# Reordering weight loads, a late scales load and the last tile's routing in a hybrid decoder step

## The reference, cut to what matters

```python
def hier_moe(m, w_router_group, w_router_expert, w_gate, w_up, w_down):
    # top-1 of 4 groups, then top-2 of its 8 experts, per token
    ...
    hg = jnp.einsum('btd,edf->btef', m, w_gate)      # 32 experts, 1024 -> 256
    hu = jnp.einsum('btd,edf->btef', m, w_up)
    hidden = jax.nn.silu(hg) * hu * gates[..., None].astype(m.dtype)
    return jnp.einsum('btef,efd->btd', hidden, w_down)

def decoder_layer(...):
    ...
    h = h + mixed
    h = h + hier_moe(rms_norm(h, g_ffn), *ffn_w)
    gate = jax.nn.sigmoid(jnp.einsum('btd,de->bte', rms_norm(h, g_ple), w_ple_gate))
    h = h + jnp.einsum('btp,pd->btd', p_i, w_ple_proj) * gate
```

## Time and profile before

| | |
|---|---|
| Median of three runs | 1237.9 us (1232.99 to 1240.14) |
| Profiled execution | 1235.65 us, span 1233.9 us |
| TensorE products busy | 1147.6 us, 93% of the span |
| TensorE weight loads | 593.5 us, 48% |
| VectorE / ScalarE / GpSimd | 407.2 / 323.6 / 144.8 us |
| Granted TensorE clock, mean | 0.971 |
| DMA | 224.17 MB, mean 182 GB/s |
| Chain that ended last | TensorE 83%, DMA 8%, VectorE 3%, ScalarE 2% |

### The profile page before, as it was taken

How to read it: one execution, slowest core, us unless ns; L and a number is a source line. 1 busy time by engine, 2 the same in 40 slices (tenths; PEclk the granted TensorE clock), 3 DMA queues, 4 the chain that set the end, 5 groups by cost and what they waited for, 6 DMA issues and landing times.

```text
span 1233.9 us, 14797 instructions
## 1 busy us (share of the span) xinstructions
PE 1147.6 (93%) x5706; PEld 593.5 (48%) x5706; DVE 407.2 (33%) x968; ACT 323.6 (26%) x635; POOL 144.8 (12%) x141
## 2 busy tenths in 40 slices
PE   6999997999999999999999998789998887889997
PEld 3444443666666665554555555324443332234443
DVE  0222223566651332132256554361111111024443
ACT  2232322677721121110111112211111100134443
POOL 0111010012220000000101111331321100000000
PEclk9999998999999999999999997899999988899999
DMA  8211013111074436334487226449999996982431
GB/s 307 58 51 51 21 39 91 48 36 35 2 217 142 118 113 171 120 120 149 150 313 265 109 83 259 166 166 410 416 418 415 410 418 257 404 310 89 156 125 39
DMA packets 69940, 224.17 MB, mean 182 GB/s; under 512 B 17822, under 2 KB 31550, under 8 KB 54000
## 3 DMA queue, kind: packets, MB, share of 16 engines
q1 hardware_dynamic: 59264, 194.26, 43.8%
q0 software_dynamic: 9888, 26.37, 5.7%
q10 hardware_dynamic: 720, 2.62, 0.5%
HBM read 196.62 MB, written 31.32 MB: 185 GB/s over the span
## 4 chain that ended last, share of the span: by engine, by line
PE 83%; DMA 8%; DVE 3%; ACT 2%; issue 2%; SPq 1%; POOL 0%; ACTq 0%; POOLq 0%; DVEq 0%
PE pair L1898 14%; PE pair L2110 13%; PE pair L2309 9%; PE pair L2173 9%; PE pair L2407 9%; DMA R<-in_w_up 6%; PE pair L2331 4%; PE pair L1967 3%; PE pair L1954 3%; PE pair L1980 3%; PE pair L2202 1%; PE pair L2029 1%; PE pair L2296 1%; PE pair L2046 1%; PE pair L2388 1%
## 5 line engine op out<-in xcount | busy, mean ns | idle before, releaser
L2309 PE MATMUL pair<-R 128*32 128x512 f32 (+2 forms) x896 | 159.8, 630 | 26.8 <-DMA R<-in_w_up 24.7
L2110 PE MATMUL pair<-R 128*128 128x352 f32 x576 | 178.6, 463 | 0.0
L1898 PE MATMUL pair<-R 128*128 128x512 f32 x384 | 171.8, 605 | 3.3 <-DMA R<-in_w_in 3.3
L2110 PEld LDWEIGHTS pair<-R 128*128 128x128 f32 x576 | 106.6, 190 | 57.9 <-issue 4.4
L1898 PEld LDWEIGHTS pair<-R 128*128 128x128 f32 x384 | 73.3, 194 | 91.0 <-issue 91.0
L2173 PE MATMUL pair<-R 128*128 128x512 f32 x256 | 115.3, 604 | 0.0
L2407 PE MATMUL pair<-R 128*128 128x512 f32 x256 | 111.5, 593 | 1.7 <-ACT R L1216 1.7
L2309 PEld LDWEIGHTS pair<-R 128*32 128x32 f32 (+2 forms) x896 | 51.9, 130 | 119.6 <-issue 115.9
L1721 DVE TENSOR_TENSOR R<-pair,R 128x256 f32<-128x256 f32 x21 | 8.9, 425 | 235.4 <-ACT R L1173 235.3
L2331 PE MATMUL pair<-R,bias 128*32 128x512 f32 (+2 forms) x448 | 76.4, 596 | 0.6 <-ACT bias L1177 0.6
L2407 PEld LDWEIGHTS pair<-R 128*128 128x128 f32 x256 | 47.9, 190 | 59.2 <-issue 59.1
(11 more groups left out here) (297 smaller groups left out, 1261.8 us busy)
## 6 DMA issues: line engine op xcount, KB each, us to landing
R<-in_w_gate SPq DMA_DIRECT2D x32, 1024.0 KB, 16.2
R<-in_w_up SPq DMA_DIRECT2D x32, 1024.0 KB, 19.3
R<-in_w_down SPq DMA_DIRECT2D x32, 1024.0 KB, 17.2
R<-in_x_prompt SPq DMA_DIRECT2D x16, 512.0 KB, 3.5
R<-in_cache_k SPq DMA_DIRECT2D x8, 1024.0 KB, 5.6
R<-in_cache_v SPq DMA_DIRECT2D x8, 1024.0 KB, 5.4
R<-y_dram SPq DMA_DIRECT2D x16, 512.0 KB, 6.6
R<-in_w_in SPq DMA_DIRECT2D x3, 2048.0 KB, 16.9
```

What stands on the lines that cost most here:

```text
L1898: last = mm(bk[4 + part][0:n, :], xTs[a.u][:, c, 0:n], wA[:, c, AD * part:AD * part + AD], start=(c == 0), stop=(c == DC - 1))
L2110: last = mm(bk[b][:, 0:n], wB[q % 2][:, c, which, :], xT[:, c, lo:lo + n], start=(c == 0), stop=(c == DC - 1))
L2309: last = mm(bk[2 + u][r, :].rearrange("p (w f) -> p w f", w=2), xgT[u][:, c, r], wgu[s][:, :, c, :], start=(c == 0), stop=(c == DC - 1))
```

## The change

The loop over loads 6 to 31 is sorted by the point at which each part's buffer comes free: a wide part has the key 2n and a down part 2n + 3, n being the last block that read the buffer, so that down(n) stands between up(n+1) and up(n+2), as on TensorE. Each part reads its expert's number by itself, so the register is read twice for each expert. The load of `gple` stands behind all expert weights. On TensorE the last tile's logits come right after its transposes, the rank after the first half of an embedding product, and the products of tile 1 move behind the count.

```diff
-        for l in range(NSTAT, NE):
+        for _, l, wide in sorted([(2 * LBEFORE[l], l, True) for l in range(NSTAT, NE)] + [(2 * LBEFORE[l] + 3, l, False) for l in range(NSTAT, NE)]):
             e = expert(l)
-            sp.wait_ge(S("gu_full"), LBEFORE[l] + 1)
-            load_wide(e, LSLOT[l])
-            sp.wait_ge(S("y_full"), 2 * LBEFORE[l] + 2)
-            load_down(e, LSLOT[l])
-            if l == NSTAT:
-                sp.wait_ge(S("routed"), 1)
-                for u in range(2):
-                    sp.wait_ge(S(f"ple_out{u}"), 16 * SAVED[u])
-                sp.dma_start(gple, I["g_ple"][0:1, :].broadcast_to([P, D])).then_inc(S("wrt_in"), 16)
+            if wide:
+                sp.wait_ge(S("gu_full"), LBEFORE[l] + 1)
+                load_wide(e, LSLOT[l])
+            else:
+                sp.wait_ge(S("y_full"), 2 * LBEFORE[l] + 2)
+                load_down(e, LSLOT[l])
+        sp.wait_ge(S("routed"), 1)
+        for u in range(2):
+            sp.wait_ge(S(f"ple_out{u}"), 16 * SAVED[u])
+        sp.dma_start(gple, I["g_ple"][0:1, :].broadcast_to([P, D])).then_inc(S("wrt_in"), 16)
         sp.wait_ge(S("gu_full"), SFINAL[4] + 1)
...
         turn_p(0)
         turn_p(1)
         router(TILES - 1)
+        logits(TILES - 1)
         pe.wait_ge(S("h_done"), 2 * PT + 4)
         pe.wait_ge(S("wpp_in"), 32)
         embed_early(0, 0)
-        logits(TILES - 1)
+        rank(TILES - 1)
         embed_early(0, 1)
         pe.wait_ge(S("p_in"), 48)
         turn_p(2)
-        embed_early(1, 0)
-        embed_early(1, 1)
-        rank(TILES - 1)
         pe.wait_ge(S("cum_done"), TILES)
         mm(bk[7][:, 0:NE], ones[:, :], r_cum[(TILES - 1) % 2], start=True, stop=True).then_inc(S("cnt_full"), 1)
-        for t in range(2, EARLY):
-            if t + 1 < EARLY:
+        for t in range(1, EARLY):
+            if 1 < t < EARLY - 1:
                 turn_p(t + 1)
             embed_early(t, 0)
             embed_early(t, 1)
```

## The result

The changed kernel takes 1217.8 us (median of 4 runs, 1213.67 to 1220.28) beside 1235.5 for the kernel before on the same chip (4 runs, 1232.41 to 1240.14): a ratio of 0.985, interval 0.9804 to 0.9897, or 18.5 us less. A repeat with six executions gave 1216.4 against 1237.4: 0.9835 (0.9803 to 0.9866), 20.4 us. The profiled execution took 1213.67 us (span 1212.0), the lowest of its four, 22.0 less than the profiled one of before. I had forecast 25, to 1210.5. Direction and range held; the size was too large by 5 to 6 us in the medians, by 3 in the pair of profiles.

What follows compares the result with a forecast made beforehand. The expert stage was taken as one weight stream with holes, costing TensorE about 32 us of waits and half clock. Rank move 8 us plus part order 17 us gave 25 us: 1210.5 us, range 1200 to 1226.

Steps and rivals of the forecast that it cites:

- The chain from there to the landed lists is 11.7 us: Before block 0, from rank's result to landed lists: 774.8 by the chain, 778.2 behind queued weights; rows 6.0 us earlier.
- the first part: Logits and rank ahead of the embedding products, so block 0 starts earlier: 8 us, ends 3 and 9.5.
- Clock up in block 0: TensorE idles only about 1.7 us before block 0, so its up-products take 7.1 us instead of 9.13: 2.0 us.
- First hole: Empty stretch of the weight stream at 802 to 832 us: 14.2 us empty from 812, about 3 stay, 11 gained.
- Second hole: Empty stretch of the weight stream at 1022 to 1042 us: 11.3 us gained, 2 reopened by load 31.
- The tail: After the last down-products, reloaded rows decide: combination 15.7 us earlier, 17.5 of the stream's 20 us left, 17 taken.
- Second part: Sorted order of weight parts with the scales last: 17 us, ends 10 and 21.
- rival d: Expert stage: down parts queue behind wide parts and TensorE waits on them; 11 us slower, 1246.7; chance 0.04.
- (a): The stream gives back its first hole only, a new wait replacing the second: 1220.7 up to 1226; chance 0.15.
- (c): The rank move gives nothing, products or small lists keeping block 0 in place: 17 us, 1218.7; chance 0.03.
- (b): Both parts reach their upper ends, TensorE alone setting the tail: 32.5 us, 1203; chance 0.12.
- (e): Early issue fills no hole in the stream; only the first part counts: 1227.7 to 1232.7; chance 0.08.

Runs made afterwards that it cites:

- the square of four kernels: Ratios to the kernel before: logits and rank early alone 0.9982; loads 4 and 5 late alone 0.9995; changed kernel 0.985; changed kernel with loads 4 and 5 late 0.9795.
- the second profile: Profile of the changed kernel run again unaltered beside the kernel before: execution 1218.26 us, median 1216.4 us, ratio 0.9835.
- order and scales: Kernel before with the sorted order of weight parts and the scales last, without the move of logits and rank: 1219.6 us, ratio 0.9875.
- loads 4 and 5 late: Changed kernel with loads 4 and 5 issued behind the small list loads and the first two gathers: 1209.3 us, ratio 0.9795.
- tail parts early: Changed kernel with 4 MB (scales, projection weights, embeddings, two gate-weight parts, two residual tiles) ahead of the last down part: 1217.8 us, ratio 0.9862.

## Why the prediction was right or wrong, point by point

- **What bounds it.** Right. The waits and the half clock in front of up-products were read as the price of the holes: 32 us. 23.0 of them went, and 9.5 us of waits are left (12 forecast), 7.71 and 1.15 of them before blocks 17 and 18, as forecast.
- **Rank's advance.** Right: 9.4 us forecast, 10.4 read, 0.6 of it an offset of the two executions.
- **"The chain from there to the landed lists is 11.7 us", the lists landing at 778.2.** This step failed, and with it the size of the first part. I let the small loads wait for the queue but kept the list stores at the duration of the idle stream, and took the small loads as landing within a microsecond of the weights. The stores took 6.89 us instead of 3.78, the loads 6.27 instead of 2.72. The lists went out only at 772.3 to 773.5 and the last landed at 780.3. Block 0's rows came 3.0 us earlier (net of the offset) in one execution and 1.6 in the other, not 6.0. On the order in the queue the Trainium skill (DMA: Bandwidth & Descriptors, section Queues, rings and completion order) was cited against this part: its ring order agrees with loads that land late, and the square of four kernels shows that 6 MB issued ahead are what the early rank runs into. That the weights delay the stores too, which leave from GpSimd's queue, no rule of order on one ring says; the rows do: 6.9 us with the weights ahead, 4.5 with them late.
- **Clock up in block 0, 2.0 us.** Followed from the same step and fell with it: idle 7.34 us instead of 1.7, 8.87 us instead of 7.1 (9.81 and 8.55 in the second profile). With the loads late the idle went and 7.07 came. So the first part was worth 2.2 us when alone (-0.2 to 4.8) and 3.3 in the first pair of profiles, about my lower end of 3 and not 8: most of the error of the whole.
- **First hole, 11 us of stream.** 9.2 (18.1 to 8.9). **Second hole, 11.3 less 2.** 5.5 (11.3 to 5.8): load 31 and the last down part reopen 5.8, not 2, as SyncE stands at 1030.89 for 12.44 us. But that hole lies behind the last up part, so no up-products wait for it: the down-products end 23.0 us earlier where I had 20 (20.3 in the second profile, from block 1 on as here). The stream thus gave back 14.7 us where I had 20, and the products nevertheless moved by my 20 or more. That the term came out is in part luck: the sum took a us of stream for a us of TensorE, and it is TensorE's row that closes, 15.1 us of waits and 7.9 of clock.
- **The tail.** The mechanism held: rows become late (22.37 us of wait), and from the end of the down-products to the combination it is 15.0 us where I had 15.1 (10.8 + 4.3). The combination starts 18.8 us earlier, counted from block 1 on, where 15.7 was forecast, the transposes 20.6 where 17.5 was. In the first profile half clock takes 2.0 us of this back (first gate products 9.13 for 7.10), which I had not counted; the second profile has none of it. Second part in all: 17 forecast, 15.4 measured alone (12.6 to 18.3), 18.1 in the first pair of profiles (22.0 less 3.9).
- **Down parts as a wait (rival d).** Did not come: no wait on them in the changed kernel. The two runs with 4 MB ahead of one down part show that this cost exists (2.96 and 4.30 us).
- **Rivals (a) and (c).** The medians, 1216 to 1218, lie nearest to (c), 1218.7: the rank's move worth next to nothing. I had given it 0.03, too little for the step with the longest chain of small transfers. (a), 1220.7 up to 1226, is not what happened; (b) and (e) neither. The part of (e) that is true is that filling one hole alone is worth little: 2.3 us for the second.
- **What would show it.** Came: no stand at 830.90, the rank's advance, no stretch near 103, shorter waits before up-products (9.5 us on up parts, 12 forecast), the combination ended by the reloaded rows, no wait on down parts, no list landed before 777. Did not come: the first gather 6 us earlier (3.9, or 3.3 net), block 0's products near 7.1 us, and 400 GB/s or more throughout from 824 on (393 at 834 to 844, 389 at 1024 to 1034). By the last of my signs of being wrong, under 410 GB/s in a full stretch, two stretches of 20 us fail (401 and 405 at 904 to 944); the slices of 30 us have 402 to 420, and the stream's mean in the sum, 416, was a little high.
- **One execution.** The forecast was set against one profile. The changed kernel's profile is the lowest of its four, and that of *order and scales* (1224.52) the highest of its four by 5 us; at the same rank product executions stand between 749.98 and 754.98. The two profiles of the changed kernel differ by 1.4 us in block 0's rows and by 2.0 in the clock of the gate products. In single profiles a term under 4 us is read from differences within a stage, not from the end, and better from two executions.

## What to carry to other kernels

When weights stream through one queue, issue each part in the order in which its buffer comes free, and keep anything that waits for another engine (the scales) out of the middle: here 15.4 us of 1235 for the two, and a good deal less for either alone. Before pulling a chain of small stores, loads and gathers forward, look what bulk transfers it will now meet, and issue those behind it: that was worth some 5 to 7 us more. A hole in a stream is worth the waits of the engine behind it less what the next stage takes back, and not its own length: look also where the reordering opens the next one.

## What the runs showed of the hardware

- The stream of one core holds 402 to 420 GB/s through six slices of 30 us each, and 392 over the 245 us of the stage with its gathers and scatters.
- Small transfers take about twice as long beside weights: list loads on the same queue 5.8 to 8.5 us in two executions of the changed kernel, 2.3 to 3.1 with loads 4 and 5 late and 1.7 to 2.8 in the kernel before; the last list store, from another queue, 6.9 us for 4.5 and 3.8.
- TensorE's granted clock after waits of 2 to 3 us is not settled by their length. In two executions of the changed kernel the first gate products ran at half clock behind waits of 2.52 and 1.72 us (9.13) and at full clock behind 2.56 and 1.74 (7.10). Up-products behind 2.47 us ran at full clock (7.09), behind 2.06 us in another kernel partly at half clock (8.77, where both shapes take 7.1 undisturbed). The first row is of the kernel with late loads 4 and 5, the second of the one with tail parts early. I draw no rule from them:

```profile
981.87 7.09 PE L2310 MATMUL pair<-R 128*64 128x512 f32 x32 [2.47 <-DMA R<-in_w_up]
```

```profile
1023.57 8.77 PE L2315 MATMUL pair<-R 128*32 128x512 f32 x64 [2.06 <-DMA R<-in_w_up]
```
